# Sample attention over paged keys: keys turned in 32x32 blocks by VectorE, score products over 32 rows on four row groups, the softmax of one sample under the values of the one before

## What is computed

```python
def mla_attend_sample(q_lat, q_pe, c_kv, k_pe, past_c, past_kpe):   # past_c (8, 2048, 256), past_kpe (8, 2048, 64)
    s_past = (einsum('bqhc,bkc->bhqk', q_lat, past_c) + einsum('bqhr,bkr->bhqk', q_pe, past_kpe)) * MLA_SCALE
    s_new = (einsum('bqhc,bkc->bhqk', q_lat, c_kv) + einsum('bqhr,bkr->bhqk', q_pe, k_pe)) * MLA_SCALE
    s_new = where(causal, s_new, -inf)
    pr = softmax(concatenate([s_past, s_new], axis=-1), axis=-1)
    return einsum('bhqk,bkc->bqhc', pr[..., :P], past_c) + einsum('bhqk,bkc->bqhc', pr[..., P:], c_kv)
```

## Time and profile before

| | |
|---|---|
| median of 3 runs (lowest to highest) | 2024.9 us (2017.25 to 2025.73) |
| span of the profiled execution | 2022.0 us |
| `mla_project`, from its first instruction | 456.2 to 507.5 us |
| `mla_prompt` | 507.5 to about 556.5 us |
| `mla_sample` | about 556.5 to 719 us |
| TensorE busy, whole span | 1864.9 us (92%) |
| VectorE, ScalarE, GpSimd busy | 694.4, 494.2, 150.8 us |

### The profile page before, as it was taken

The page is one execution under the profiler, slowest core; times in us unless marked ns, Lnnn a source line. Parts: engine busy times, 40 slices in busy tenths (PEclk is TensorE's granted clock), DMA queues, the critical chain, the costliest instruction groups (busy, mean ns, idle before and its releaser), DMA issues.

```text
span 2022.0 us, 36262 instructions
## 1 busy us (share of the span) xinstructions
PE 1864.9 (92%) x14871; PEld 1259.8 (62%) x14871; DVE 694.4 (34%) x1340; ACT 494.2 (24%) x856; POOL 150.8 (7%) x197
## 2 busy tenths in 40 slices
PE   6999997988899989899999999999999999999994
PEld 5999997865655579878545554445555445554442
DVE  4437765555445443465331111111111111111113
ACT  4445554331223232363131101101110000000001
POOL 0000003200223100000100000000000000000000
PEclk8999998998999999999999999999999999999997
DMA  8545531123334386256879999999999999999995
GB/s 227 153 125 146 131 91 23 47 49 113 105 104 137 95 252 165 94 156 203 320 297 417 424 422 424 426 420 369 425 424 422 421 425 401 407 427 421 422 424 193
DMA packets 212005, 543.34 MB, mean 269 GB/s; under 512 B 44604, under 2 KB 168606, under 8 KB 185200
## 3 DMA queue, kind: packets, MB, share of 16 engines
q1 hardware_dynamic: 203666, 532.97, 69.4%
q0 software_dynamic: 7792, 8.53, 1.9%
q10 hardware_dynamic: 438, 0.32, 0.1%
HBM read 524.86 MB, written 28.06 MB: 273 GB/s over the span
## 4 chain that ended last, share of the span: by engine, by line
DMA 29%; PE 19%; issue 1%; DVE 1%; DVEq 0%
DMA w_expert<-in_w_up_dram 27%; PE p_u L2970 7%; PE p_y L2986 4%; PE p_g L2970 3%; PE p_xg L2938 3%; DMA w_expert<-in_w_down_dram 1%; PE p_xgT L2953 1%; PE p_g L2945 0%; DVE w_expert L3140 0%; DVE w_expert L3131 0%; PE p_xgT L2959 0%; PE p_xgT L3045 0%; PE p_xg L3045 0%; PE p_y L2993 0%; PE p_g L3045 0%
## 5 line engine op out<-in xcount | busy, mean ns | idle before, releaser
L2970 PE MATMUL p_u<-w_expert,xgT 128*64 128x256 f32 x2048 | 236.3, 384 | 38.9 <-DMA w_expert<-in_w_up_dram 38.9
L2970 PE MATMUL p_g<-w_expert,xgT 128*64 128x256 f32 x2048 | 232.0, 379 | 0.9 <-DVE xgT L3070 0.9
L2970 PEld LDWEIGHTS p_u<-w_expert,xgT 128*64 128x64 f32 x2048 | 146.8, 138 | 121.4 <-DMA w_expert<-in_w_up_dram 48.9
L2986 PE MATMUL p_y<-w_expert,hidT 128*64 128x512 f32 x960 | 219.2, 599 | 1.2 <-DMA w_expert<-in_w_down_dram 1.2
L2970 PEld LDWEIGHTS p_g<-w_expert,xgT 128*64 128x64 f32 x2048 | 147.1, 137 | 87.6 <-issue 18.4
L2938 PE MATMUL p_xg<-low,slot_sel 128*64 128x512 f32 x768 | 177.1, 596 | 0.0
L2986 PEld LDWEIGHTS p_y<-w_expert,hidT 128*64 128x64 f32 x960 | 67.2, 137 | 126.9 <-issue 124.9
L3075 DVE CAST row<-rowf 128x1 int32<-128x1 f32 x32 | 4.9, 154 | 356.0 <-POOLq L3212 356.0
L3160 ACT ACTIVATE act_g<-p_g 128x256 f32<-128x256 f32 x32 | 12.3, 384 | 451.3 <-PE p_u L2970 451.3
L3209 POOL DMA_INDIRECT x_dram<-y_slots,row x31 | 48.2, 1555 | 883.2 <-DVE y_slots L3086 883.2
L2938 PEld LDWEIGHTS p_xg<-low,slot_sel 128*64 128x64 f32 x768 | 52.4, 137 | 79.4 <-issue 73.6
(11 more groups left out here) (602 smaller groups left out, 2560.6 us busy)
## 6 DMA issues: line engine op xcount, KB each, us to landing
w_expert<-in_w_gate_dram SPq DMA_DIRECT2D x64, 2048.0 KB, 23.6
w_expert<-in_w_up_dram SPq DMA_DIRECT2D x64, 2048.0 KB, 25.1
w_expert<-in_w_down_dram SPq DMA_DIRECT2D x60, 2048.0 KB, 21.2
w_in_raw<-in_w_in_dram SPq DMA_DIRECT2D x32, 1024.0 KB, 5.7
lat<-in_cache_kv_latent_dram SPq DMA_DIRECT2D x128, 128.0 KB, 2.0
ho_raw<-in_w_out_dram SPq DMA_DIRECT2D x12, 1024.0 KB, 6.5
tables_sb<-in_w_out_dram SPq DMA_DIRECT2D x4, 1024.0 KB, 7.5
mem_k_s<-in_cache_mem_k_dram SPq DMA_DIRECT2D x8, 512.0 KB, 7.3
```

The costliest lines, as they stand in the source:

```text
L2970: mm = pe.matmul(acc[SL * h:SL * h + SL, 0:FF // 2], xgT[:, t, g // 2, :], w[g][:, FF * t + FF // 2 * h:FF * t + FF // 2 * h + FF // 2], s ...
L2986: mm = pe.matmul(p_y[SL * h:SL * h + SL, 512 * b:512 * b + 512], hidT[:, j, g, :], tile, start=(g == 0 and j == 0), stop=(g == 1 and j == 1))
```

## The change

It does six things.

1. **Loading.** Page numbers are turned into row numbers in `mla_project` (8 x page + eighth of the page), and POOL loads a sample with two indirect DMAs, `gather_pages`: a partition takes 16 consecutive tokens, 16 KB of latents and 4 KB of rotary keys. Three samples are started in `mla_prompt`.
2. **Turning keys.** DVE transposes `lat` and `rope` in 32x32 blocks from SBUF to SBUF (`turn_keys`): 10 instructions of 128 x 512 a sample. Partition group `a` (32 partitions) of `kT[:, c, :]` then holds features 32c to 32c+31 of that group's 512 keys.
3. **Scores.** Each of the 10 feature blocks is 8 products with 32 rows, 64 columns and 256 keys: 4 row groups `a` by 2 halves, into four PSUM banks by row group. The queries must lie on all four groups: `q_own` is made by POOL and spread by 24 SBUF to SBUF DMAs in `mla_prompt` (`S.q_parts`).
4. **Softmax.** The reduction over 1024 scores is one instruction, and the short ones after it are fewer. ACT writes the probabilities so that their transposes come out in the order of the tokens.
5. **Order.** PE forms the scores of sample b, then turns the probabilities and takes the values of sample b-1. ACT, not DVE, copies `probT` and scales the rows; adding the halves is a product with `eye2` (L1869 of the changed kernel).
6. **Places.** The hardware loop is gone (the 8 samples are written out), `q_lat` lives until `heads_out`, and the first block of `w_out` is loaded into its place after the last scores.

The core of the diff (renamed semaphores and SBUF allocations are left out):

```diff
@@ mla_project, SP and POOL
+                for r in range(8):
+                    sp.dma_start(numbers[NPG * r:NPG * r + NPG, :], d['page_table'].rearrange("b p -> p b"), allow_slow_non_contiguous=True).then_inc(numbers_in, 16)
...
+                pool.tensor_scalar(numbers_f[:, :], numbers_f[:, :], 8.0, S.table("sub_row"), ALU.mult, ALU.add).then_inc(row_steps, 1)
@@ mla_prompt, SP and POOL
-                for b in range(NBUF - 1):
-                    pages_by_sp(d, S, sp, b)
+                sp.wait_ge(q_apart, 2)
+                for a in range(4):
+                    rows = slice(32 * a, 32 * a + 32)
+                    for c in range(4):
+                        sp.dma_start(S.q_pairs[c][rows, :], q_own[32 * c:32 * c + 32, :, :].rearrange("p c n -> p (c n)")).then_inc(q_spread, 16)
...
+                for b in range(NBUF):
+                    gather_pages(pool, d, S, b)
@@ a sample's pages
+def gather_pages(pool, d, S, b):
+
+    last_row = NPHYS * 8 - 1
+    for cache, dst, signal in ((d['cache_kv_latent'][0], S.lat, S.lat_in), (d['cache_k_rope'][0], S.rope, S.rope_in)):
+        pool.indirect_dma_start(out=dst[b % NBUF][:, :, :].rearrange("p k n -> p (k n)"), out_offset=None, in_=cache.rearrange("i (r k) n -> (i r) (k n)", r=8),
+                                in_offset=bass.IndirectOffsetOnAxis(ap=S.page_rows[:, b:b + 1], axis=0), bounds_check=last_row, oob_is_err=False).then_inc(signal[b % NBUF], 16)
@@ mla_sample, POOL
-                pages_by_pool(d, S, pool, NBUF - 1)
                 for b in range(NBUF, NB):
-                    pool.wait_ge(made, b + 1)
-                    pool.nop(nofuse=True)
-                    pages_by_pool(d, S, pool, b)
+                    pool.wait_ge(made, b - NBUF + 1)
+                    gather_pages(pool, d, S, b)
@@ mla_sample, PE
+                def past(b, parts):
+                    for c in parts:
+                        pe.wait_ge(key_turned, NCB * b + c + 1)
+                        if c == 0 and b:
+                            pe.wait_ge(exped, b)
+                        for half in range(2):
+                            for a in range(4):
+                                quad = slice(32 * a, 32 * a + 32)
+                                ins = pe.matmul(p_s[64 * half:64 * half + 64, a, :], S.q_parts[c][quad, 64 * b:64 * b + 64], kT[quad, c, 256 * half:256 * half + 256], start=(c == 0), stop=(c == NCB - 1))
+                        ins.then_inc(key_used, 1)
...
+                for b in range(NB):
+                    past(b, range(0, 6))
+                    if b >= 2:
+                        turn_rows(b - 2)
+                    past(b, range(6, NCB))
+                    new_keys(b)
+                    if b:
+                        turn_probabilities(b - 1)
+                        values(b - 1)
@@ mla_sample, DVE
+                def turn_keys(b, parts):
+                    for c in parts:
+                        if c == 0:
+                            dve.wait_ge(S.lat_in[b % NBUF], 16 * (b // NBUF + 1))
+                        if c == 8:
+                            dve.wait_ge(S.rope_in[b % NBUF], 16 * (b // NBUF + 1))
+                        if b:
+                            dve.wait_ge(key_used, NCB * (b - 1) + c + 1)
+                        src = lat[b % NBUF][:, :, 32 * c:32 * c + 32] if c < 8 else rope[b % NBUF][:, :, 32 * (c - 8):32 * (c - 8) + 32]
+                        dve.transpose(kT[:, c, :].rearrange("p (k n) -> p k n", n=32), src).then_inc(key_turned, 1)
...
+                turn_keys(0, range(NCB))
+                for b in range(NB):
+                    if b >= 2:
+                        store(b - 2)
+                    largest(b)
+                    if b:
+                        sums(b - 1)
+                    if b + 1 < NB:
+                        turn_keys(b + 1, range(NCB))
@@ mla_sample, ACT
+                queries(0)
+                for b in range(NB):
+                    if b >= 2:
+                        scale_rows(b - 2)
+                    if b:
+                        copies(b - 1)
+                    exponentials(b)
+                    if b + 1 < NB:
+                        queries(b + 1)
@@ build
-                S.raw_out = late_table.rearrange("p (t n) -> p t n", t=DT)
+                S.raw_out = S.q_lat[:, :, :, :].rearrange("p c h n -> p (c h n)")[:, 0:D].rearrange("p (t n) -> p t n", t=DT)
```

More of the change, by code:

```diff
@@ L77, in tables @@
     put("centre", (p == q) - (p // 64 == q // 64) / 64)
+    put("sub_row", p // NPG)
     rot = np.zeros((128, 128))
@@ L1798, in mla_sample @@
-        ring = [p_t[0], p_t[1], p_pt[:, 0:512], p_pt[:, 512:1024]]
-        NI = 12
-        KEEPS = ((2, 3, 4, 5, 7, 9, 11), (0, 1, 6, 8, 10))
-        half_scored = sem("s_half_scored")
-        def keeper(k):
-            e = 0 if k in KEEPS[0] else 1
-            return e, KEEPS[e].index(k) + 1
-        def samples(eng, first, body):
-            first()
-            with eng.Fori(0, NB // NBUF) as it:
-                for par in range(NBUF):
-                    body(NBUF * it + par, par, it)
-            for b in range(NB // NBUF * NBUF, NB):
-                body(b, b % NBUF, b // NBUF)
+        stat = sb("stat_s", [128, 2, 10]); o_rows = sb("o_rows", [128, KVL])
@@ L1924, in _ @@
-                for _ in range(NBUF):
-                    pe.nop().then_inc(made, 1)
-                samples(pe, first, body)
-            def keep(eng, copy, who, b, some):
-                for k in KEEPS[who][some]:
-                    eng.wait_ge(turned, NI * b + k + 1)
-                    if k < 8:
-                        ins = copy(kT[:, :, 256 * k:256 * k + 256], ring[k % 4][:, :].rearrange("p (c n) -> p c n", c=2))
-                    else:
-                        ins = copy(kpT[:, 512 * (k - 8):512 * (k - 8) + 512], ring[k % 4][0:64, :])
-                    ins.then_inc(kept[who], 1)
+                for b in range(NB):
[7 more added lines that the diff above has]
+                        values(b - 1)
@@ L1966, in body @@
[L1966 to L1971 removed]
+                    step(dve.scalar_tensor_tensor(st(3), st(0), st(1), st(2), ALU.max, ALU.max))
+                    dve.tensor_scalar(st(4), st(3), -MLA_SCALE, None, ALU.mult)
@@ L1975, in body, with store @@
                     step(dve.reciprocal(st(9), st(8)))
-                    step(dve.tensor_copy(st(9, 1), st(9)))
-                    dve.wait_ge(made, NBUF + b + 1)
-                    dve.tensor_scalar(o_rows[:, :], p_o[:, 0:KVL], stat[:, 9:10], None, ALU.mult).then_inc(rows, 1)
+                    dve.tensor_copy(st(9, 1), st(9)).then_inc(inverted, 1)
+                def store(b):
                     dve.wait_ge(o_turned, b + 1)
-                    src = p_n[:, 256:512].rearrange("p (c half n) -> p c half n", c=2, half=2)
@@ L1996, in _ @@
+                sums(NB - 1)
+                store(NB - 2)
+                store(NB - 1)
             @block.scalar
```

270 lines of the change are left out of this document (106 added, 164 removed).

## The result

The changed kernel takes 1974.7 us (median; 1974.1 to 1982.4), the kernel before beside it 2024.6: a ratio of 0.977, 95% interval 0.975 to 0.979. Predicted were 1969, within 1957 to 1996. Both are inside the range, and their runs do not overlap; most of what follows is about the 13 us between them.

What follows compares the result with a forecast made beforehand. PE was taken to bound the sample stage, before and after; its period falling from 18.59 to 12.15 us made the stage 106.8 us instead of 162.6, so 2024.9 - 55.8 = 1969 us, range 1957 to 1996.

Steps and rivals of the forecast that it cites:

- PE, scores anew: Sample-stage scores: eight products side by side take 0.51 us (0.46 to 0.60), so 5.1 us a sample against 5.8 before.
- the two-at-a-time rival: Score products: row groups stream only two at a time, 0.213 us a product, period 24.1, kernel 2060 us; chance 0.06.
- DVE, transposes anew: Key transposes on DVE in the sample stage: ten of 128 x 512 at 0.69 us (0.64 to 1.08), 6.9 a sample.
- the slow-rate rival: Key transposes on DVE take 1.04 to 1.08 us each, DVE sets a period of 15.0, kernel 1993 us; chance 0.14.
- The new period: Sample stage: PE stays the bound, 12.15 us a sample instead of 18.59; DVE needs 11.35.
- the cover: Sample stage: PE's period exceeds DVE's by 0.8 us; with a transpose over 0.77, DVE sets the period.
- Ends: Sample stage: first scores 8.9 us, next interval 10.9, six periods 72.9, tail 14.1; sum 106.8 against 162.6, -55.8 us.
- Loading: Sample loads: 8.6 to 10.9 us to landing, 9.4 available; at most 0.3 us a sample, taken as no cost.
- The ring of buffers: Three sample buffers: 9.4 us from a buffer coming free to DVE wanting its data; could set a 12.45 us period.
- the prediction's smaller estimate, 6.8: Loading the latents: 6.8 us from the skill's 2.0 us and 436 GB/s, hidden as well.
- What I cost at nothing: POOL's copies (2.6 us) and three sample loads with 24 spreading DMAs (37 us), hidden in `mla_prompt`'s 49 us; other small loads.
- something else: Remaining causes, such as a barrier made later by the spreading or code fetched for the written-out loops; chance 0.03.

Runs made afterwards that it cites:

- set 3: Three kernels on one chip, beside the kernel before: changed kernel unchanged, 1961.8 us; its query-spreading DMAs late, 1962.6; these and the prompt's page DMAs late, 1963.6.
- sets 2 to 4: Eight versions, each set on another chip: rope pages only 1956.8 us, half the rows 1959.0, spread late 1962.4, one row group 2229.2; three at 1961.8 to 1963.6; two row groups 2013.5.
- the version with both late: Changed kernel with the 24 query-spreading DMAs and the six indirect page DMAs of the prompt stage waiting for the first value products: 1963.6 us, ratio 0.971.
- set 1: Four versions of the changed kernel on one chip: no sample-stage page reload 1961.3 us, direct DMAs instead 1965.8, later gather 1979.1, prompt's page DMAs late 1970.2.

## Why the prediction was right, and where it was off

By its own steps, on the undisturbed execution (the changed kernel in set 3) and on the one of the result:

- **PE, scores anew: right, over-priced.** I took 0.51 us for eight products, bounds 0.46 to 0.60. They took 0.43, which is below my lower bound and is what I had named as the floor of the streaming: eight tiles cost nothing on top. Shown by the runs with fewer row groups, at full clock: 0.43 on four, 0.86 on two, 1.84 on one. That settles the two-at-a-time rival, whose eight products would have taken 1.7. The Trainium skill, TensorEngine Tiling (Array Packing), "Key Properties", has different tiles load and multiply in parallel; the trace agrees, with 0.43 us for eight and 0.86 for eight on half the tiles.
- **DVE, transposes anew: over-priced.** 0.69 taken, bounds 0.64 and 1.08, 0.60 measured from start to start. The dense form was the right neighbour, the slow-rate rival (1.04) is refuted; the overlap of one with the next was missing in the sum.
- **The new period: right in kind, 12.15 said, 11.74 measured**; the scores were 10 x 0.08 = 0.8 less than summed, the rest 0.4 more. DVE waits 2.25 us a period for PE, but more than half of that is PE's last block and the new keys, which stand behind DVE's last transpose in any case. What it can spare is seen in set 3: transposes that began 0.80 us late cost nothing, those that began 1.27 late (615.59) made a period of 12.01 for 11.74. So the cover is 1.0 us; I had reckoned 0.8.
- **Ends.** First scores read 7.8 us behind the start of the stage (8.9), next interval 10.7 (10.9), six periods 70.7 (72.9), tail 14.4 (14.1): 103.6 us for 106.8 predicted.
- **Loading: right in what it costs, thinner than I said.** The ring of buffers was put at 9.4 us and landing at 8.6 to 10.9. In set 3 the latents set VectorE going 9.1 us behind the issue, and it had waited 0.80: it wanted them at 8.3, not at 9.4, and it waited in three of the five periods. Of the period 11.74 nothing was lost to it but once (12.01). The latents landed 8.0 us behind the issue in the execution of the result and 9.1 in set 3 (medians), so the prediction's smaller estimate, 6.8, was too short.
- **What I cost at nothing: wrong in the execution of the result.** "both lie in `mla_prompt`'s 49 us, which PE sets" held in the sets 2 to 4 (first scores 49.6 to 49.9 us behind the prompt's start, but for the version with both late), not there (53.4): 3.6 us. The step that failed is that an indirect DMA's issue costs only POOL's own time, 1.56 us (it took 1.00). In the sample stage the same step missed 5 x 1.93 = 9.7 us. Together 13.3; the medians of the same kernel with and without differ by 13.0.

So 1969 came close by luck, as two errors met: 3.2 us too much for the stage itself, and up to 13.3 too little for what the gather can do to other engines. The two together would put the result at 1979, and it is 1974.7; the first alone would put set 3 at 1966, and it is 1961.8. Both are some 4 us faster than the stages explain. That lies outside the two stages or in the spread of the runs (the kernel before: 2017 to 2026 us), and nothing here tells which. In my prediction a hold-up of other engines by the gather had no rival of its own; "something else" had 0.03.

**What is shown and what stays open.** Shown on one chip: without indirect DMAs in the sample stage no hold-up, with the same bytes by direct DMAs none, with the DMA moved it moves along, and that in the prompt stage goes when the page DMAs are moved. Shown over the sets: the same code can run without any hold-up. Not every indirect DMA does it: behind the 31 of the expert stage (L3171), in the same execution, no two weight loads of PE start more than 0.21 us apart in the next 3.5 us. What differs between the sets, the chip or where a load puts the program, was not tried and is open, as is by what way an issue on POOL reaches PE, and why in the prompt stage it appears at VectorE and ScalarE. Two sets showed hold-ups (the result's and set 1) and three did not, too few to say which is usual. Delaying the prompt's page DMAs brings the first scores 2.8 to 5.2 us forward against the other versions of its set, where there are hold-ups; with both kinds late nothing is gained where there are none. In set 3, the only one with the changed kernel beside them, no version beat it.

## What to carry to other kernels

Price small tiles by their row groups: where a 128-row product becomes four of 32 rows, four row groups running together give back all of it; on two the products took twice as long, on one four times, and in both cases the clock could fall to half on top (for two samples, and for most of the stage). Price a software-issued DMA not only on the engine that issues it: look at what the others do in the 3 us behind it, and run an unchanged kernel in more than one set before a cause is put down to an edit.

## What the runs showed of the hardware that I had not expected

- The granted clock stood at 0.50 with a PE that was never idle (5.00 busy of 5.00), while its products used one of four row groups, and rose to 1.00 beside the value products over 128 rows; being busy did not keep the clock up.
- An indirect DMA issued by POOL can hold PE's weight loads up three times by 0.51 us, beginning 0.8 us behind it, in every one of five periods, and in another set, with the same code, not at all.
- 32x32 transposes of 128 x 512, written densely, start every 0.60 us though each is 0.675 long, where the strided ones of the kernel take 1.08.
